# Two modulation pieces move ahead of Hyena's first projection tile, and the tables of its last way back ahead of four pieces' loads

## The reference, cut to what matters

```python
sh1, sc1, g1, sh2, sc2, g2 = jnp.split((silu_c @ w_mod[l] + b_mod[l])[:, None, :], N_MOD, axis=-1)
h = modulate(x, norm1_g[l], sh1, sc1)
zl_hy, zl_gla, zl_gdn = split_last(h @ w_in, IN_SIZES)

def hyena_mix(z, n_seg, seg_len, conv_w, conv_b, filt, d_skip):
    u = (short_conv(z, conv_w, n_seg, seg_len) + conv_b).astype(F32)
    v, x1, x2 = jnp.split(u, 3, axis=-1)
    l = u.shape[1]
    filt_f = jnp.fft.rfft(filt, axis=0)
    y = v
    for o, gate in enumerate((x1, x2)):
        conv = jnp.fft.irfft(jnp.fft.rfft(y, n=2 * l, axis=1) * filt_f[None, :, o], n=2 * l, axis=1)[:, :l]
        y = gate * (conv + d_skip[o].astype(F32) * y)
    return y.astype(z.dtype)

# second block, layers 0 and 1
mod_x = jnp.split((sc @ w_ada[l] + b_ada[l])[:, None, :], 3, axis=-1)
mod_c = jnp.split(scc @ w_ada[l] + b_ada[l], 3, axis=-1)
```

## Time and profile before

| | us |
|---|---|
| median of 3 runs | 3682.08 |
| lowest, highest | 3678.49, 3686.81 |
| the profiled execution, its device time | 3682.67 |
| its span, from the first to the last instruction | 3680.9 |
| TensorE's matmuls busy | 3573.4 (97%) |
| VectorE busy | 1726.2 (47%) |
| ScalarE busy | 972.0 (26%) |
| mean granted TensorE clock | 0.989 |

### The profile page before, as it was taken

The page is one execution under the profiler, slowest core; times in us unless marked ns, Lnnn a source line. Parts: engine busy times, 40 slices in busy tenths (PEclk is TensorE's granted clock), DMA queues, the critical chain, the costliest instruction groups (busy, mean ns, idle before and its releaser), DMA issues.

```text
span 3680.9 us, 48256 instructions
## 1 busy us (share of the span) xinstructions
PE 3573.4 (97%) x19396; PEld 2261.0 (61%) x19396; DVE 1726.2 (47%) x3669; ACT 972.0 (26%) x1822; POOL 625.4 (17%) x564
## 2 busy tenths in 40 slices
PE   7999999999989999999999999999999999999999
PEld 4578967654844444444444588857654569866654
DVE  4878863274742333333435845423531464423531
ACT  5234422221103100000016213313541312313531
POOL 3002310231001322122224013110001102211001
PEclk9999999999989999999999999999999999999999
DMA  7201130453441111111103124120020413210021
GB/s 248 99 11 40 36 110 29 152 184 121 138 171 46 46 46 43 38 46 46 46 25 117 67 71 107 29 73 12 1 92 0 174 36 97 76 61 24 1 86 46
DMA packets 190444, 266.04 MB, mean 72 GB/s; under 512 B 27309, under 2 KB 133400, under 8 KB 189584
## 3 DMA queue, kind: packets, MB, share of 16 engines
q1 hardware_dynamic: 177728, 198.89, 17.3%
q0 software_dynamic: 12496, 64.06, 4.6%
HBM read 228.11 MB, written 34.81 MB: 71 GB/s over the span
## 4 chain that ended last, share of the span: by engine, by line
PE 89%; DVE 6%; ACT 2%; issue 1%; DMA 1%; POOL 0%; DVEq 0%; SPq 0%; ACTq 0%; POOLq 0%
PE ps L3379 19%; PE ps L3250 10%; PE ps L1039 9%; PE ps L4341 7%; PE ps L1061 6%; PE ps L4634 4%; PE ps L4811 3%; PE ps L1126 2%; PE ps L4291 2%; PE ps L4868 2%; PE ps L4851 2%; PE ps L3447 1%; PE ps L2942 1%; PE ps L1820 1%; PE ps L1836 1%
## 5 line engine op out<-in xcount | busy, mean ns | idle before, releaser
L3379 PE MATMUL ps<-big 128*128 128x512 f32 x1624 | 697.1, 592 | 0.0
L3379 PEld LDWEIGHTS ps<-big 128*128 128x128 f32 x1624 | 308.6, 190 | 388.4 <-issue 385.3
L1039 PE MATMUL ps<-big 128*128 128x512 f32 (+1 forms) x1056 | 403.6, 543 | 0.0
L3250 PE MATMUL ps<-big 128*128 128x512 f32 (+1 forms) x896 | 361.0, 564 | 4.6 <-issue 2.6
L1039 PEld LDWEIGHTS ps<-big 128*128 128x128 f32 x1056 | 200.2, 191 | 197.2 <-issue 191.0
L3250 PEld LDWEIGHTS ps<-big 128*128 128x128 f32 x896 | 170.3, 191 | 190.3 <-issue 184.6
L3572 DVE SCALAR_TENSOR_TENSOR big<-ps,big 128x512 f32<-128x512 f32 x212 | 159.1, 751 | 242.7 <-PE ps L3379 208.7
L4341 PE MATMUL ps<-big 128*128 128x256 f32 x1152 | 252.6, 379 | 0.0
L4341 PEld LDWEIGHTS ps<-big 128*128 128x128 f32 x1152 | 217.2, 190 | 29.3 <-issue 0.7
L1061 PE MATMUL ps<-big 128*128 128x256 f32 (+1 forms) x1344 | 229.0, 332 | 0.0
L1061 PEld LDWEIGHTS ps<-big 128*128 128x128 f32 x1344 | 208.0, 191 | 22.2 <-ACT big L2345 2.5
(11 more groups left out here) (515 smaller groups left out, 5242.3 us busy)
## 6 DMA issues: line engine op xcount, KB each, us to landing
big<-in_w_mlp SPq DMA_DIRECT2D x32, 1024.0 KB, 5.4
big<-in_w_in SPq DMA_DIRECT2D x29, 1024.0 KB, 5.5
big<-in_w_mod SPq DMA_DIRECT2D x24, 1024.0 KB, 7.5
big<-in_w_ada SPq DMA_DIRECT2D x24, 1024.0 KB, 5.4
big<-us_scratch SPq DMA_DIRECT2D x72, 256.0 KB, 4.5
hs_scratch<-big POOLq DMA_DIRECT2D x3, 5120.0 KB, 18.6
xs_scratch<-big POOLq DMA_DIRECT2D x16, 640.0 KB, 3.4
big<-hs_scratch POOLq DMA_DIRECT2D x9, 1024.0 KB, 8.2
```

Of the source, the lines that this page charges most:

```text
L1039: t = e.matmul(b[:, 0:n], wv[:, k, 128 * m:128 * m + 128], K.hT[:, k, t0:t0 + n], start=(k == 0), stop=(k == 7))
L3250: t = e.matmul(b[:, 0:n], wv[:, k, c:c + 128], cat[:, k, t0:t0 + n], start=(k == 0), stop=(k == 7))
L3379: t = e.matmul(z, w[:, k, c], y, start=(first and k == 0), stop=(k == nk - 1), skip_group_check=not first)
```

## The change

In `HyProj`, SP requests two pieces ahead of the first tile's table and one behind it, where it requested three behind it; TensorE runs two pieces at the stage's start and one between the tile's halves, where it ran three between them. In `Hyena`, SP requests both c_idft tables of the last way back after two of the six pieces that were spread around them, and the other four after both; TensorE runs two pieces between the two last back runs and one after the second, where it ran three between them. The number of pieces, loads and matmuls is the same, and so is what is computed.

```diff
@@ HyProj.sync
     def sync(self, e):
+        self.mods.sync_take(e, 2)
         self.cm_sync(e, self.K.A["w_in"][0], 0, 2)
-        self.mods.sync_take(e, 3)
+        self.mods.sync_take(e, 1)
         self.head.sync(e)
         e.wait_ge(*self.at("hT in", "hy", 0))
         self.cm_sync(e, self.K.A["w_in"][0], 256, 4)
@@ HyProj.tensor
         pr, tr = Banks(K, (0, 1, 2, 3)), Banks(K, (4, 5))
+        self.mods.tensor_take(e, 2)
         used, wv = K.W.use(e, 256)
@@
         e.wait_ge(*self.at("hT half in", "hy", 0))
         first(range(0, 4))
-        self.mods.tensor_take(e, 3)
+        self.mods.tensor_take(e, 1)
         e.wait_ge(*self.at("hT in", "hy", 0))
         first(range(4, 8))
@@ Hyena.sync
         self.mat(e, "c_dft", 1)
-        self.mods.sync_take(e, 3)
+        self.mods.sync_take(e, 2)
         self.mat(e, "c_idft", 0)
-        self.mods.sync_take(e, 3)
         self.mat(e, "c_idft", 1)
+        self.mods.sync_take(e, 4)
```

## The result

| | us, median | lowest to highest | runs | against before |
|---|---|---|---|---|
| before | 3682.89 | 3678.49 to 3686.81 | 6 | |
| changed | 3696.26 | 3695.07 to 3793.75 | 6 | 1.0038, interval 1.0027 to 1.0049 |
| changed, measured again beside before (3683.11) | 3696.11 | 3693.51 to 3697.38 | 5 | 1.0035, interval 1.0023 to 1.0047 |

What follows compares the result with a forecast made beforehand. TensorE was taken as the bound, busy 97% of the span and 89% of the chain. Gains of 3.48 us at the projection's start and 0.02 at the last way back made 3.50, from 3682.08 to 3678.6 us; range 3674 to 3685.

Steps and rivals of the forecast that it cites:

- Part A: Start of Hyena's projection: two pieces moved ahead of the tile's wait for hT; 3.48 us gained, or 1.81.
- Part A, the placement: Start of Hyena's projection: two pieces of work go into TensorE's 3.79 us idle, 1.81 us gained.
- Part A, the clock: First half of Hyena's first tile: the shortened idle no longer lowers TensorE's clock, 1.67 us gained.
- the stretch at 712: Earlier stretch, 1.32 us busy in 3.00 us, granted clock 1.00 throughout; cited for the clock holding at the tile.
- Rival 1: Hyena's first tile: the clock falls in the shortened idle too; 1.83 us gained in all, 3680.3 us; chance 0.18.
- The collision: Before L1126: two SP weight tables requested beside block 1 of hT; it lands at 810.8 to 813.2, no wait.
- rival 2: Before L1126: block 1 lands at 815.4, TensorE waits 2.2 us, 1.3 us gain remains, 3680.8 us; chance 0.14.
- Part B: Hyena's last way back: back run starts 0.95 us earlier, late piece costs 0.93; net 0.02 us gained.
- rival 3: Last back run gets the higher clock sooner: 8.90 or 7.11 us instead of 10.14; 3677.3 or 3675.6 us; chance 0.16.
- place B: Hyena's last way back, where the last back run waits for c_idft and for VectorE's Z.
- something outside both places: Anything beyond the two edited places, such as the spread of the runs; chance 0.04.
- place A: Start of Hyena's projection, where TensorE idles 3.79 us until the first half of block 0 of hT is back.

Runs made afterwards that it cites:

- part A with the fill: Kernel before plus the HyProj edit, and a third piece moved ahead of Hyena's last transposes: 3676.70 us, ratio 0.9983.
- part A alone: Kernel before plus only the HyProj edit: 3693.31 us, median of 12; five runs from 3676.04 to 3680.54, seven from 3691.36 to 3701.84.
- the kernel before, less work: Kernel before with two of the 16 matmuls of Hyena's first tile left out: 3696.17 us, 3694.84 to 3697.80, all five runs.
- both parts, extra matmuls: Changed kernel plus eight extra matmuls of 128 rows after the third of Hyena's taps: 3692.15 us.
- both parts: The changed kernel itself, no further edit, timed again beside the kernel before: 3696.11 us, ratio 1.0035.
- both parts, held up: Changed kernel with the transposes of Hyena's first convolved unit done twice: 3682.53 us, ratio 0.9998.
- the kernel before, one matmul less: Kernel before with one matmul of Hyena's first tile left out: 3681.60 us, median of 12; eight runs from 3675.70 to 3682.19, four from 3695.18 to 3701.40.
- part B, SP's order only: Kernel before with both c_idft tables requested ahead of four pieces, all three pieces still between the last back runs: 3681.51 us, ratio 0.9998.
- part B alone: Kernel before plus only the two Hyena hunks: tables ahead of four pieces, last piece after the last back run: 3682.67 us, ratio 0.9997.
- both parts, filled: Changed kernel with a third piece moved ahead of Hyena's last transposes, out of the taps: 3677.43 us, ratio 0.9983.
- part A filled, SP's order: Kernel before plus the HyProj edit, third piece ahead of Hyena's last transposes, c_idft tables requested earlier, last three pieces unmoved: 3676.75 us, ratio 0.9984.
- the kernel before, filled: Kernel before with only the third piece moved ahead of Hyena's last transposes: 3680.68 us, ratio 0.9992.

## Why the prediction was wrong

**Part A, the placement: right.** The two pieces lie in the idle, no load is late, and L1126 isn't delayed. 1.46 us came of the 1.81; the rest is mostly that the first half of hT let the tile start 6.29 us after its request, not 6.03 (0.26), and that the one piece left between the halves takes 1.00 us, not 0.90.

**Part A, the clock: wrong.** I took the 1.67 us on the strength of the stretch at 712. In six of the seven records the tile took 8.80 us after an idle of 2.02 to 2.46 us; in one, after 2.49, it took 7.11. Rival 1 was the likelier case. The stretch at 712 was no safe ground either: in the record of part A with the fill, the same stretch of work has an idle of 2.09 us instead of 1.68, and the clock falls in the microsecond from 713 (0.65, then 0.50). Having this wrong costs 1.7 us of forecast, not 13.

**The collision: no wait, as forecast, but with less room than I took.** The copy landed after 8.5 us. The forecast had taken 5.5 to 7.9, rival 2 10.1. It was in at 814.0, 1.7 us ahead of L1126, which came late because the clock had fallen at the tile. Where the clock held (part A with the fill), the copy took 8.3 us from 805.78 and was in at 814.1, and L1126 started at 814.45: 0.4 us of room. The estimate from the Trainium skill (DMA: Bandwidth & Descriptors, Queues, rings and completion order), by its turns among queues, was 2.4 us later than 5.5; it measured 3.0 and 2.8 later, so the trace agrees in kind.

**Part B: the wait and the price right, the run's clock open.** Z ends the wait, and the gain is small and taken back. The run started 0.15 us after Z (0.05 forecast), and the turn came 1.80 us after the run (1.71 forecast). The longer idle didn't hurt: with both tables early the run took 8.75 to 9.55 us in the seven records that have them so. That doesn't make rival 3 right. In the six records with SP's old order, the kernel before among them, the same run took 8.59 to 10.15 us, so the 10.14 of the one record that I read was near the long end of what the unedited place does. The time shows no difference.

**The step that failed** is the sentence that closes part A: from the tile to place B the chain goes on from TensorE's work, "and all waits move with it". The waits did. But I had priced the clock only where the edit touched an idle stretch, and treated all between as a block that slides; "something outside both places" had a chance of 0.04 and no mechanism. It slides by 0.9 us, and at its end stands a place where TensorE's clock can be lost: 1.46 us of idle, eight records of transposes, then 16.67 us of taps, on half the rows but for two pieces. In the kernel before, no run is plainly of the slower kind: 91 reach up to 3689.68, and the record has 1.00. But the slower runs of part A alone begin at 3691.36, so the times don't exclude a rare fall there. Moved earlier, it falls there, and then the half-row matmuls don't bring it back. Its price is read off directly: 31.32 - 16.67 = 14.65 us in the taps and their pieces, of which the earlier start gives back 0.94. The granted clock of the whole run says it once more: 0.986 against 0.989.

That timing is the cause and not the pieces is shown from both sides: less work ahead of the place in the kernel before gives the loss in all five runs (1.72 us less) or in four of 12 (0.86 us, 6.11 from start to start instead of 6.97); 0.97 us more work in the changed kernel takes it away in ten of 11. The long idle is needed: with a piece in it and 0.59 us left, none of 33 runs of the three filled versions with part A has the loss. And the length of the low stretch is due to the taps: matmuls on all rows and columns in their midst end it. The pieces, with weights of 128 rows but 32 columns, ran at 0.50 for 1.93 us each and didn't.

A general rule was at hand. The Trainium skill (TensorE: Matmul & The Clock Gate, Part 1: The HAM clock gate) says that the slow state is the default and that activity releases it. The trace agrees for the tile and for the runs of 128 rows; for the taps it shows that being busy isn't enough: TensorE was busy for 32.00 of 32.00 us from 906 to 938 at 0.50.

**What separates the executions.** The time since the start of the span doesn't: part A alone reached the taps at 905.21 and lost the clock, the kernel before reached them at 905.24 and kept it. What does is the time since the clock's own last fall, the one in place A. In the kernel before it fell at 798.94, within this microsecond:

```profile
...
798.00:799.00 1.00, 0.75 (x2) 0.49 (x3) 0.93 (x3) 0.00 (x0) 0.00 (x0) 0.97 1.02 386
...
```

With part A alone it fell at 800.00, 1.06 us later, and the transposes start at the same time of the span:

```profile
...
799.00:800.00 1.00, 0.03 (x1) 0.07 (x1) 0.97 (x2) 0.00 (x0) 0.00 (x0) 1.00 1.04 393
800.00:801.00 1.00, 1.00 (x2) 0.48 (x3) 0.93 (x3) 0.00 (x0) 0.00 (x0) 0.50 1.02 350
...
904.05 1.23 PE L2795 MATMUL ps<-big 128*128 128x128 f32 x8 [1.45 <-DVE big L1208]
905.21 10.28 PE L2976 MATMUL ps<-big 64*128 64x512 f32 x12
...
```

All records with a fall in place A, its time read to 0.1 us or better from short windows (us):

| record | fall in place A | the eight transposes start | between | clock in the taps |
|---|---|---|---|---|
| the kernel before, less work | 803.40 | 906.94 | 103.54 | falls |
| both parts, extra matmuls | 797.59 | 901.22 | 103.63 | falls |
| both parts | 799.40 | 903.14 | 103.74 | falls |
| part A alone | 800.00 | 904.05 | 104.05 | falls |
| both parts, held up | 802.55 | 907.11 | 104.56 | stays |
| the kernel before, one matmul less | 797.65 | 902.37 | 104.72 | stays |
| the kernel before | 798.94 | 904.08 | 105.14 | stays |
| part B, SP's order only | 798.68 | 904.02 | 105.34 | stays |
| part B alone | 798.41 | 904.19 | 105.78 | stays |
| both parts, filled | 804.03 | 907.73 | 103.70 | stays |
| part A filled, SP's order | 798.05 | 901.79 | 103.74 | stays |
| the kernel before, filled | 798.93 | 904.34 | 105.41 | stays |

In the nine records without the fill, the clock falls up to 104.05 us and stays from 104.56 on. This is what "earlier" means here: earlier against the clock's own changes, whose place shifts from one execution to the next. Two filled records lie where every unfilled one lost the clock, and kept it, so the piece in the idle does guard it. The order was read from the records afterwards; no run was made to test it, and the filled record without a fall in place A can't be placed in the table.

**What stays open.** Not all of the filled versions' gain is accounted for: 1.46 us of part A and 0.87 of the piece in the idle make 2.3 of the 6.3 measured. Part A alone already gains 5.1 us in its five runs without the loss. The granted clock of the 33 filled runs is 0.989 to 0.992, in the median 0.991, against 0.989 in the median of the 91 of the kernel before, so the rest may be other places where the clock fell less; that is argued only.

## What to carry to other kernels

Before a block of work is moved in time, go through all of it for places where TensorE idles, however shortly, ahead of matmuls that use part of the rows, and not only through the lines that the edit touches. In these records a clock lost there stayed lost as long as that work lasted; what kept it was filler in the idle directly ahead, and what brought it back was a few us of full-size matmuls. And a time with two modes, or a loss that grows when work is taken away, is a reason to read the granted clock stretch by stretch before reading any wait.

## What the runs showed of the hardware

- The granted clock fell to 0.50 after an idle of only 1.46 us ahead of light work (transposes, then matmuls of 64 rows), with TensorE busy when it fell; ahead of full-row work, idles of 2.02 to 2.46 us did it in six records and 2.49 us didn't in one.
- Matmuls of 64 rows, with two pieces among them, held a clock of 1.00 for 17 us (905 to 922 before), but didn't raise one of 0.50 in over 30 us. Matmuls of 128 rows raised it about 3 to 4 us after they began.
- Whether the clock fell went by the time since its own fall some 104 us before: at most 104.05 us in the four records in which it fell, at least 104.56 in the five in which it stayed.
- Less work can cost time: 1.72 us of matmuls taken away made the kernel 12.6 us slower, and 0.97 us added made the changed kernel 13.6 us faster.
- A copy of 1 MB from scratch beside two table loads of 1 MB landed after 8.5 us (8.3 in a second record) instead of 5.5.
